# Scores of the two heads of a pair in the two row halves of the TensorE array, with the key bias as a pass of its own

## What is computed

```python
q = rms_norm(q, q_gain);  k = rms_norm(k, k_gain)          # per head, over its 64 features
moba:    logits = q k^T / 8 - slope * (i - j),     causal
fox:     logits = q k^T / 8 + cum_i - cum_j,       causal   # cum: running sum of log sigmoid(f)
dilated: three branches (128,1), (512,4), (2048,16), mixed by their denominators
p = softmax(logits);  o = p v
y = rms_norm(o per group) * out_gain (fox also * sigmoid(g_fox));  x + concat(y) @ w_out
```

## Time and profile before

| | us |
|---|---|
| median of 3 runs (lowest, highest) | 1568.57 (1568.27, 1569.46) |
| time of the profiled execution | 1569.62 |
| its span, first to last instruction | 1567.7 |
| PE busy in the span | 1502.1 (96%) |
| PE weight loads | 1296.0 (83%) |
| DVE, ACT, POOL busy | 845.5, 617.2, 267.5 |
| mean granted TensorE clock | 0.984 |
| 936 to 1182 us (attention): PE busy of 246.00 | 240.19 |
| DVE, ACT busy there | 163.04, 130.16 |
| granted clock there | 1.00 |
| chain that ended last, by engine | PE 85%, DVE 7%, POOL 4%, ACT 2%, issue 1% |

### The profile page before, as it was taken

How to read it: one execution, slowest core, us unless ns; L and a number is a source line. 1 busy time by engine, 2 the same in 40 slices (tenths; PEclk the granted TensorE clock), 3 DMA queues, 4 the chain that set the end, 5 groups by cost and what they waited for, 6 DMA issues and landing times.

```text
span 1567.7 us, 23464 instructions
## 1 busy us (share of the span) xinstructions
PE 1502.1 (96%) x9229; PEld 1296.0 (83%) x9229; DVE 845.5 (54%) x1229; ACT 617.2 (39%) x920; POOL 267.5 (17%) x272
## 2 busy tenths in 40 slices
PE   7978999999979999999997999999999999999998
PEld 7977999999968888988985677888886888888887
DVE  5778734357455543553455536776845534434344
ACT  5547655543233221231233334646534422323230
POOL 2665100000024622550542000000100000000000
PEclk9989999999989999999998999999999999999999
DMA  5211211223212232233232221111122232222221
GB/s 190 82 42 54 69 54 55 68 81 137 94 41 82 94 107 81 94 95 103 84 101 80 67 72 63 44 39 55 41 81 95 84 104 94 94 94 94 93 94 67
DMA packets 36006, 128.03 MB, mean 82 GB/s; under 512 B 4460, under 2 KB 4588, under 8 KB 35792
## 3 DMA queue, kind: packets, MB, share of 16 engines
q1 hardware_dynamic: 34464, 122.18, 23.6%
q10 hardware_dynamic: 864, 4.33, 0.7%
q0 software_dynamic: 592, 0.30, 0.1%
HBM read 124.68 MB, written 2.10 MB: 81 GB/s over the span
## 4 chain that ended last, share of the span: by engine, by line
PE 85%; DVE 7%; POOL 4%; ACT 2%; issue 1%; DMA 0%; SPq 0%; DVEq 0%; POOLq 0%; ACTq 0%
PE ps L1695 72%; PE ps L2028 2%; PE ps L2052 2%; PE ps L1873 1%; PE ps L1715 1%; POOL phase_tmp L1564 1%; PE ps L2039 1%; PE ps L1823 1%; DVE h_lo L860 1%; DVE w_lo L847 1%; PE ps L2006 1%; DVE x L860 1%; POOL acc L1564 1%; POOL conv_tmp L1653 1%; POOL phase L1564 1%
## 5 line engine op out<-in xcount | busy, mean ns | idle before, releaser
L1695 PE MATMUL ps<-h_hi,w_hi 128*128 128x264 f32 (+1 forms) x1768 | 512.7, 339 | 37.9 <-DVE h_lo L860 17.6
L1695 PE MATMUL ps<-h_lo,w_hi 128*128 128x264 f32 (+1 forms) x1768 | 495.1, 330 | 0.0
L1695 PE MATMUL ps<-h_hi,w_lo 128*128 128x264 f32 (+1 forms) x1768 | 493.6, 329 | 0.0
L847 DVE TENSOR_TENSOR w_lo<-w_raw,w_hi 128x1024 fp32r<-128x1024 f32 (+2 forms) x227 | 291.1, 1283 | 182.2 <-ACT w_hi L349 180.9
L1695 PEld LDWEIGHTS ps<-h_hi,w_hi 128*128 128x128 f32 x1768 | 301.5, 190 | 89.0 <-issue 35.3
L1695 PEld LDWEIGHTS ps<-h_lo,w_hi 128*128 128x128 f32 x1768 | 298.8, 189 | 33.8 <-issue 6.0
L1695 PEld LDWEIGHTS ps<-h_hi,w_lo 128*128 128x128 f32 x1768 | 298.5, 189 | 29.9
L349 ACT ACTIVATE w_hi<-w_raw 128x1024 fp32r<-128x1024 f32 (+2 forms) x227 | 233.2, 1035 | 200.0 <-PE ps L1695 199.2
L1695 PE MATMUL ps<-mlp_lo,w_hi 128*128 128x512 f32 x256 | 100.9, 394 | 0.0
L1695 PE MATMUL ps<-mlp_hi,w_hi 128*128 128x512 f32 x256 | 100.3, 392 | 0.0
L1695 PE MATMUL ps<-mlp_hi,w_lo 128*128 128x512 f32 x256 | 99.4, 388 | 0.0
(11 more groups left out here) (293 smaller groups left out, 1945.8 us busy)
## 6 DMA issues: line engine op xcount, KB each, us to landing
w_raw<-w_units SPq DMA_DIRECT2D x227, 512.0 KB, 3.3
x<-x_t ACTq DMA_DIRECT2D x1, 2112.0 KB, 7.8
out<-out_tile SPq DMA_DIRECT2D x8, 256.0 KB, 2.0
x<-x_t ACTq DMA_DIRECT2D x3, 528.0 KB, 8.8
x<-x_t ACTq DMA_DIRECT2D x2, 264.0 KB, 4.3
consts<-consts SPq DMA_DIRECT2D x1, 320.0 KB, 6.6
b_step<-ssm_b SPq DMA_DIRECT2D x1, 256.0 KB, 10.2
c_step<-ssm_c SPq DMA_DIRECT2D x1, 256.0 KB, 10.8
```

The source lines that it names most:

```text
L847: Dv.do(v.tensor_tensor(wlo[:, s % RING, 0:w], raw[:, s % RING, 0:w], f32(whi[:, s % RING, 0:w]), ALU.subtract), lo_ready)
L1695: ins = mm(o, wt[:, s % RING, w], xt[:, kx, c0:c0 + n], start=(b == 0 and a == 0), stop=(b == len(blocks) - 1 and a == 2))
```

## The change

Scores. Queries and keys of a pair are kept as one tile of 128 rows each (`q_pair`, `k_pair`): rows 0 to 63 head 0, rows 64 to 127 head 1. One scaling operation on DVE replaces two on 64 rows. `scores(i)` now does both heads, in two groups of blocks, t = 1 and 3, then t = 0 and 2. Each group has three steps: the key bias, as an fp32r matmul that picks two rows (high and low part) out of 64 by a selection matrix; the masks, as before; the products. The bias and product matmuls of head 0 take the upper 64 rows of the array and those of head 1 the lower 64 (`tile_position=(64 * hh, 0)`); the masks take all 128 rows.

Bias. The 16 DMAs of bias rows and the two memsets of ones are gone. All rows are prepared once: POOL builds eight selection columns and brings in the bias of all heads (five DMAs), ACT makes the rounded copy and the selection matrix, DVE the low parts (two operations on 16 rows).

Order. There is one softmax period a pair. Iteration i on PE is now W0(i), V(i-2, both), S(i-1, both), T0(i), W1(i), P(i-1, both), T1(i); ACT and DVE are rearranged to it. The whole diff without the definitions of tiles, the set-up of the bias on POOL and the host's layout of its input:

```diff
-BANK_DONE = (3, 2, 3, 4)
+BANK_DONE = (4, 1, 4, 2)
+    T_ORDER = (1, 3, 0, 2)
...
@@ ScalarE
+            A.do(dn.activation(selr[:, :, :], esel.unsqueeze(2).to_broadcast([P, KT, P]), ACT.Copy), sem("masks_ready"))
...
             qk_rsqrt(0, 1)
+            act.wait_ge(sem("fox_in"), 64)
+            A.do(dn.activation(kbr[:, :], kbias[:, :], ACT.Copy), sem("bias_hi"))
...
             for i in range(1, KT):
                 last = i == KT - 1
+                if i >= 2:
+                    pt_copy(i - 2, 0)
+                    qk_rsqrt(i - 1, 1)
+                    pt_copy(i - 2, 1)
                 if last:
                     moba_gain(0)
-                if i >= 2:
-                    pt_copy(i - 2, 1)
                 qk_square(i, 0)
                 if last:
                     moba_gain(1)
-                exps(i - 1, 0)
                 split_hi(qk_unit(i, 0) + LOOK)
                 if i == KT - 3:
                     group_squares(0)
                 if i == KT - 2:
                     group_squares(1)
+                exps(i - 1, 0)
+                exps(i - 1, 1)
                 qk_rsqrt(i, 0)
                 if i == KT - 2:
                     group_rsqrt(2, 0, 2)
-                if not last:
-                    split_hi(qk_unit(i, 1) + LOOK)
+                split_hi(qk_unit(i, 1) + LOOK)
                 qk_square(i, 1)
...
-                qk_rsqrt(i, 1)
-                exps(i - 1, 1)
-
-
+
+
+            for m in range(4):
+                y_hi(m)
+            pt_copy(KT - 2, 0)
+            y_hi(4)
+            qk_rsqrt(KT - 1, 1)
+            pt_copy(KT - 2, 1)
             split_hi(U_OA + 2)
             split_hi(U_OA + 3)
-            pt_copy(KT - 2, 1)
             exps(KT - 1, 0)
+            exps(KT - 1, 1)
...
@@ VectorE
-                dst = (qa, ka)[w][i % 2]
-                for hh in range(2):
-                    a = slice(64 * hh, 64 * hh + 64)
-                    g = cols[a, COL[("q_gain", "k_gain")[w]] + i:COL[("q_gain", "k_gain")[w]] + i + 1]
-                    stt(dst[0:64, hh, :], qr[w][a, :], g, sq[w][a, 0:SEQ], M, M, sem("aug_ready"))
+                stt((qa, ka)[w][i % 2][:, :], qr[w][:, :], col(("q_gain", "k_gain")[w], i), sq[w][:, 0:SEQ], M, M,
+                    sem("aug_ready"))
...
+            dve.wait_ge(sem("bias_hi"), 1)
+            for p in (32, 96):
+                tt(kbr[p:p + 16, :], kbias[p:p + 16, :], f32(kbr[p:p + 16, :]), S_, sem("bias_lo"))
...
             for i in range(1, KT):
                 last = i == KT - 1
+                if i >= 2:
+                    qk_ms(i - 1, 1)
+                    pt_copy(i - 2, 0)
+                    pt_copy(i - 2, 1)
+                    qk_norm(i - 1, 1)
                 qk_evac(i, 0)
+                split_lo(qk_unit(i, 0) + LOOK)
                 if i >= 2:
-                    pt_copy(i - 2, 1)
-                maxima(i - 1, 0)
+                    attn_out(i - 2, 0)
                 if last:
                     fox_gate(2)
                 if i >= 2:
                     attn_out(i - 2, 1)
+                maxima(i - 1, 0)
                 if last:
                     fox_gate(3)
-                qk_ms(i, 0)
-                split_lo(qk_unit(i, 0) + LOOK)
                 if i == KT - 2:
                     group_ms(0, 2)
...
+                maxima(i - 1, 1)
+                qk_ms(i, 0)
+                split_lo(qk_unit(i, 1) + LOOK)
                 if i == KT - 2:
                     group_norm(1, 0, 2)
...
+                qk_evac(i, 1)
+                qk_norm(i, 0)
+
+
+            fox_gate(4)
+            for m in range(4):
+                y_lo(m)
+            qk_ms(KT - 1, 1)
+            y_lo(4)
+            pt_copy(KT - 2, 0)
+            pt_copy(KT - 2, 1)
+            qk_norm(KT - 1, 1)
...
@@ TensorE
+            def scores(i):
...
+                rows_of = (slice(0, 64), slice(64, 128))
+                for ts in (T_ORDER[:2], T_ORDER[2:]):
+                    if ts[0] == 0 and i:
+                        pe.wait_ge(sem("attn_done"), 2 * i)
+                    for t in ts:
+                        bank, c = QB[t]
+                        w = P * (t + 1)
+                        for hh in range(2):
+                            mm(PS[:, 2 + 3 * hh + bank, c:c + w], selr[rows_of[hh], i, :], kbr[rows_of[hh], 0:w],
+                               start=(t != 2), stop=True, skip_group_check=True, tile_position=(64 * hh, 0))
+                    for t in ts:
...
+                            if 2 * i + hh < N_MOBA + N_FOX:
+                                mm(PS[:, 2 + 3 * hh + bank, c + w - P:c + w], identr[:, :], maskr[:, :], start=False, stop=True,
+                                   skip_group_check=True)
+                            else:
+                                for part in range(2):
+                                    mm(PS[:, 2 + 3 * hh + bank, c:c + w], identr[:, :], dilr[:, part, P * (3 - t):SEQ],
+                                       start=False, stop=True, skip_group_check=True)
+                    for t in ts:
...
+                            r = rows_of[hh]
+                            ins = mm(PS[:, 2 + 3 * hh + bank, c:c + w], qa[i % 2][r, P * t:P * t + P], ka[i % 2][r, 0:w],
+                                     start=False, stop=True, skip_group_check=True, tile_position=(64 * hh, 0))
+                    ins.then_inc(sem("qk_mm"), 1)
...
                 if i >= 2:
-                    p_transposes(i - 2, 1)
+                    values(i - 2, 0)
...
-                scores(i - 1, 0)
+                if i >= 2:
+                    values(i - 2, 1)
...
-                if i >= 2:
-                    values(i - 2, 1)
+                scores(i - 1)
...
                 p_transposes(i - 1, 0)
-                scores(i - 1, 1)
-                values(i - 1, 0)
+                p_transposes(i - 1, 1)
                 qk_stat(i, 1)
...
             out_part(0)
+            values(KT - 2, 0)
+            values(KT - 2, 1)
+            scores(KT - 1)
             pe.wait_ge(sem("qms_ready"), 2 * KT)
             out_part(1)
-            p_transposes(KT - 2, 1)
-            scores(KT - 1, 0)
-            values(KT - 2, 1)
             out_part(2)
+            p_transposes(KT - 1, 0)
+            p_transposes(KT - 1, 1)
             out_part(3)
-            p_transposes(KT - 1, 0)
-            scores(KT - 1, 1)
             values(KT - 1, 0)
+            values(KT - 1, 1)
             out_part(4)
             out_part(5)
-            p_transposes(KT - 1, 1)
-            values(KT - 1, 1)
             out_part(6)
             out_part(7)
```

More of the change, by code:

```diff
@@ L278, in build @@
     r2c = small[:, 0:20]
+    esel = small[:, 300:300 + KT]
     nm, rsum, rinv = (small[:, 32 + 8 * j:40 + 8 * j] for j in range(3))
@@ L690, in exps @@
                     act.wait_ge(sem("pv_mm"), h - 1)
-                for t in range(4):
+                for t in T_ORDER:
                     act.wait_ge(sem("max_ready"), 4 * h + BANK_DONE[t])
@@ L784, in _ @@
             pt_copy(KT - 1, 0)
-            exps(KT - 1, 1)
+            pt_copy(KT - 1, 1)
             split_hi(U_OA + 6)
             split_hi(U_OA + 7)
-            pt_copy(KT - 1, 1)
             group_squares(2)
@@ L1346, in maxima @@
                 b = 2 + 3 * hh
-                dve.wait_ge(sem("qk_mm"), h + 1)
                 if i:
                     dve.wait_ge(sem("p2_ready"), 4 * (h - 1))
-                for t in range(4):
+                for t in T_ORDER:
+                    if t in (T_ORDER[0], T_ORDER[2]):
+                        dve.wait_ge(sem("qk_mm"), 2 * i + 1 + T_ORDER.index(t) // 2)
                     bank, c = QB[t]
@@ L1460, in _ @@
             split_lo(U_OA + 3)
-            pt_copy(KT - 2, 1)
+            attn_out(KT - 2, 0)
+            attn_out(KT - 2, 1)
+            maxima(KT - 1, 0)
+            maxima(KT - 1, 1)
             out_part(1)
-            maxima(KT - 1, 0)
-            attn_out(KT - 2, 1)
             split_lo(U_OA + 4)
@@ L1468, in _ @@
             pt_copy(KT - 1, 0)
+            pt_copy(KT - 1, 1)
             out_part(3)
-            maxima(KT - 1, 1)
+            split_lo(U_OA + 6)
             attn_out(KT - 1, 0)
-            split_lo(U_OA + 6)
+            attn_out(KT - 1, 1)
             out_part(4)
             split_lo(U_OA + 7)
-            pt_copy(KT - 1, 1)
             out_part(5)
-            attn_out(KT - 1, 1)
             out_part(6)
@@ L1661, in _ @@
             pool.dma_start(dil[:, :], dil_in).then_inc(sem("dil_in"), 16)
-            pool.wait_ge(sem("fox_ready"), 1)
-            for i in range(KT):
-                if i >= 2:
[L1665 to L1672, removed]
+            Po.do(g.tensor_tensor(esel, ident[:, 0:2 * KT:2], ident[:, 32:32 + 2 * KT:2], A_))
+            Po.fence()
+            Po.do(g.tensor_tensor(esel, esel, ident[:, 65:65 + 2 * KT:2], A_))
+            Po.fence()
```

(12 more changed lines are left out.)

57 lines of the change are left out of this document (17 added, 40 removed).

## The result

The changed kernel takes 1572.07 us (median of 12 runs, 1570.04 to 1573.23) against 1568.99 us for the kernel before on the same chip (12 runs): ratio 1.0019, 95% interval 1.0011 to 1.0026. So the change costs 3 to 4 us, where +4.2 was forecast. The profiled execution took 1570.28 us, its span is 1568.5; it is one of the quickest of the twelve, with a granted clock of 0.988 where most have 0.985 or 0.986.

What follows compares the result with a forecast made beforehand. Attention was taken as bound by PE's column time. PE gain -4.8, T1 waits +7.8, `out_part(0)` +2.4, waits gone -1.5 make +3.9 us (exact walk +4.5); taken +4.2, median 1572.8 us, 8-in-10 range 1565 to 1578.

Steps and rivals of the forecast that it cites:

- Time and sign: Whole kernel: median 1572.8 us, +4.2; chances slower 0.58, same 0.28, faster 0.14.
- Column time of scores: S on PE: overlap gives 2.1 us a pair, bias takes 0.6, six shape changes 1.2; PE gains 4.8 in all.
- rival 4: S: row halves of 64 don't run together, S 7.5 us, +25, 1594 us; chance 0.05.
- Rivals 2 and 3: S: shape change at half cost, 1570.4 us, chance 0.12; matmuls start in strict order, 1576.2 us, chance 0.08.
- The wait of T1: Attention loop: T1 waits 1.2 us in i = 2 to 5; 7.8 us summed over i = 1 to 7.
- Why T1 waits: ACT chain to T1: table load held behind the first maximum, cost 0 to 1.29 us, taken as 1.29.
- rival 1: ACT: table load runs ahead of the wait, T1's operand there at 10.67, -3.3, 1565.3 us; chance 0.13.
- The turning point: Chain to T1: rival 1's faster case decides once it is shorter by about 0.75 us an iteration.
- `out_part(0)`: Behind i = 7: waits for `y_lo`, first block 2.1 us after T1, fifth costs 0.3 more: 2.4 us.
- The sum: All terms: -4.8 + 7.8 + 2.4 - 1.5 = +3.9 us; walking periods with exact handovers +4.5; taken +4.2.
- What goes: Last V's wait on `pt_copy` (about 1.3 us) and about 0.2 idle before `group_tile(2)` to T0(7) go: -1.5.

Runs made afterwards that it cites:

- e7: Changed kernel with the whole-array masks ahead of the bias in each group of S, four shape changes a pair instead of six: 1569.46 us.
- e4: Changed kernel with bias and products of both heads in the upper 64 rows, head 1 computed from head 0's data: 1591.41 us.
- after: The changed kernel itself, without further edits: 1572.07 us.
- e2: Changed kernel with square ahead of `split_hi` on ACT, evacuation and `qk_norm` ahead of `split_lo` on DVE: 1575.51 us.
- e1: Changed kernel with one more single-column exponential on ACT ahead of exps(i-1, 0), so the table load has no maximum to wait for: 1571.46 us.
- e5: e2 with `group_norm` moved ahead of `qk_norm(i, 0)` on DVE in the last but one iteration: 1567.08 us.
- e6: e5 with low parts ahead of `qk_norm(7, 0)` on DVE and `out_part` units reordered as cover on PE: 1561.81 us, run again 1563.14.
- e10: The changed kernel run again without edits, on another chip: 1572.26 us, against 1568.21 for the kernel before.
- e3: Kernel before with its two DVE memsets of ones moved to POOL: 1566.65 us against 1568.70.
- e9: Changed kernel with four memsets of one row x 512 put back on DVE where the kernel before has its two: 1573.54 us.
- e8: e6 and e7 together: 1560.76 us, run again 1560.55 us.

## Why the prediction was right, step by step

- **Time and sign.** 1572.8 was forecast, 1572.07 and 1572.26 came. The mechanism is the one named: PE's work falls, and new waits cost more than it gives.
- **Column time of scores: right, the gain a little too large.** S of a FoX pair was to be 4.75 us instead of 5.40. It is 4.57 from the first bias matmul on, and the change of shape ahead of that stands in V: 4.50 us, against 4.38 in e7, where no change follows. With it S is 4.69, by six changes at 0.17 instead of 0.2. The working has two slips of its own: four masks stand in it at 0.38 us where its price of 0.11 gives 0.44, and its three terms (2.1 less 0.6 less 1.2) make 0.3 and not 0.65; the rest would be masks that got cheaper, which it doesn't name. The overlap is whole (e4: +2.8 us on S without it; rival 4 said 7.5 us for S, and it is 7.36). Rivals 2 and 3, S of 4.1 or 5.5, are out: putting both heads into one half lengthens the first group's products by 1.30 us (e4), all of one head's stream (0.43 + 0.86), so in after the second head adds nothing, where strict order would have added 0.44. The strict start order that the Trainium skill states (TensorE: Matmul & The Clock Gate, Part 3) doesn't hold between row tiles here: at line 1849 of before the kernel has two products on one row tile ahead of two on the other, and in the trace the eight matmuls start in four pairs 0.013 us apart, from 201.58 on, one of each tile. Without waits the period is 24.2 us (e2) against 24.76 (2 x 12.38) before: -0.55 a FoX pair. For a dilated pair it is 25.97 (e2, T1 at 1069.39 and 1095.36) against 26.37 (before, T at 1075.90 and 1102.27): -0.40. P costs 0.16 us more now that T follows it and not a mask. So PE gains 4.0 us in all, where 4.8 was forecast.
- **The wait of T1: right in size and place.** 1.2 us were walked for i = 2 to 5; start to start, P's last transpose to T1 is 1.28 us there against 0.11 without a wait, so 1.17. It is about 0.9 in i = 1 as said, 1.67 in i = 6 (1.9 said), none in i = 7 (0.2 said): 7.2 against 7.8. The period was to be 25.4 us and is 25.49. What the walk left out is 0.1 us behind each wait: T1 takes 1.12 us instead of 1.02.
- **Why T1 waits: half right.** The table load does stand behind the wait for the first maximum, at its full price: idle 5.3 us, then 1.28 us of load (the case whose cost had been bounded by 0 and 1.29). But **rival 1 was wrongly worked out.** It said that without the load T1's operand is there 1.29 us sooner. The prediction itself has the second group's maxima at 2.9 against 3.1 us, just in time. With ACT 1.3 us sooner they would be 1.1 late, and 0.2 is all that can be won. e1 shows it: 0.25 us a period. The turning point "shorter by 0.75 us" holds as a sum (six waits of 0.75 make 4.5); the load alone could never reach it. Taking the splits out of the chain does (e2, e5).
- **`out_part(0)`: right, but for the clock.** 2.1 us for the first block was said; it is 1.95 of idle. e6 shows the reason by taking it away. The sum has no term for the clock: in e10 the matmuls behind this wait run at 1.2 GHz for 3 us, and its attention stretch is 1.4 us longer than that of after.
- **What goes: right.** The last V starts without a wait; `out_part(3)` covers `pt_copy`.
- **The missed term.** The change takes two memsets of one row each away, and the prediction has them nowhere, not even among what it costs at nothing. They stood on DVE ahead of an evacuation that PE waited for: 1.24 us of PE idle (1.4 start to start) at 935.08, just ahead of the stretch from 936 on that I had read. It goes with the change (e3, e9): -1.4. In the profiles the attention stretch itself grew by 5.0 us, from the last group-wide statistics in the prologue (942.87 before, 939.74 after) to the output transposes (1178.19, 1180.09): 235.3 and 240.35. The sum said 3.9 and 4.5 for it. Two misses explain most of that: PE gains 0.8 less than forecast, and the 0.1 behind each of six waits makes 0.6, while the waits themselves come to 0.6 less; the last tenths are not assigned. So +5.0 - 1.4 = +3.6 by these two places, between the two measured +3.1 and +4.05. The whole spans of the two profiles differ by only 0.8 us (1567.7, 1568.5). The other 2.8 lie outside both places, where the trace of before has the lower granted clock (0.93 against 0.95 from 800 to 900 us, 0.83 against 0.91 from 1170 to 1190).
- **How much of it was luck.** The mechanism was seen, but that 4.2 came within 1.1 us of both results is in part luck: costs too small and a gain not seen met, and one fall of the clock, which the sum leaves out, is worth 1.4 us.

## What to carry to other kernels

Work that leaves the bounding engine is a gain only if the cover that it gave to others isn't needed; walk the other engines' chain to the next operand of that engine in both versions, over one period. Where two operands arrive within some tenths of each other, removing the first to be seen gains only their distance, so work out each rival with the other one in place. Price every instruction of a diff by what stands behind it in its queue, a memset of one row too, and move small operations that release another engine (here `group_norm`) to the head of their queue.

## What the runs showed of the hardware

- **A wait of PE can cost several times its length, or nothing more.** Gaps are start to start here. In e2 a gap of 3.47 us was followed by 15 us of work at clock 0.50 (1.2 of 2.4 GHz): 2.1 us more wait than e5 cost 9.5. Ahead of `out_part(0)`, 3.03 us were followed by some 3 us at that level in e2 and e5. There 2.5 us were followed by 3 us of it in e1 and e10 and by none in after, e7 and e9, and e10 is the same kernel as after. In the prologue a gap of 2.27 us at some 940 us stands in every profile; behind it the clock fell in e3 and e8 (0.59 from 942 to 946 us) and in no other. So one profile doesn't tell what such a wait costs.
- **A table load can be held up by a wait.** In after it starts at 1012.96, behind 5.31 us of idle for a maximum; with one exponential of a single column (0.20 us) ahead of it, it starts at 1008.14 (e1). The exponential behind it in after has two waits. Where it has one, the load ran ahead of the wait (963.53).
- **Two heads' fp32 streams of 64 rows each overlap wholly** in the two row halves: 0.99 us for four products (eight matmuls) that take 2.29 in one half (e4).
- **A change between row tiles and whole array costs 0.17 us** (e7: two changes fewer, 0.34 us).
- **A memset of one row of 1024 floats holds DVE for 0.91 us** (before), of 512 for 0.48 (e9): it takes half as long for half the length, though only one row is written.
